# A recurrent unit moved into the projection before it and between the attention's units, and one softmax map handed to ScalarE

## The reference

```python
# block 0: x = x + gate * even_mixer(modulated rms_norm(x))
q, k, v, g_a, x_b, g_b = split(h @ w_in)            # 512 columns each
a_out = diff_attention(q, k, v, t5_table, lam, ...) # 4 heads; softmax(map 0) - lam * softmax(map 1)
b_out = bidir_rglru(x_b, ...)
y = concat([a_out * silu(g_a), b_out * silu(g_b)]) @ w_out

def bidir_rglru(x, ...):
    xc = conv4(x) + conv_b                          # 4 taps along the tokens
    gate_a, gate_x = sigmoid(xc @ w_a + b_a), sigmoid(xc @ w_x + b_x)   # both directions
    log_a = -8 * gate_a * softplus(-lam)
    a, mult = exp(log_a), sqrt(-expm1(2 * log_a))
    u = mult * gate_x * xc
    return forward_scan(a[0], u[0]) + backward_scan(a[1], u[1])   # h = a * h + u

# block 1: odd_mixer: q, k, v, g = split(h @ w_in); 16 heads of windowed attention with a
# softmax over 256 masked, biased scores; (out * silu(g)) @ w_out
```

## Time and profile before

| | us |
|---|---|
| three runs | 2048.07, 2049.44 (median), 2052.09 |
| profiled execution: time, span | 2052.9, 2051.1 |
| busy PE, DVE, ACT, POOL | 1916.6, 1396.5, 689.6, 114.3 |
| mean granted clock of TensorE | 0.970 of full speed |

### The profile page before, as it was taken

How to read it: one execution, slowest core, us unless ns; L and a number is a source line. 1 busy time by engine, 2 the same in 40 slices (tenths; PEclk the granted TensorE clock), 3 DMA queues, 4 the chain that set the end, 5 groups by cost and what they waited for, 6 DMA issues and landing times.

```text
span 2051.1 us, 28124 instructions
## 1 busy us (share of the span) xinstructions
PE 1916.6 (93%) x10810; PEld 1661.7 (81%) x10810; DVE 1396.5 (68%) x2096; ACT 689.6 (34%) x938; POOL 114.3 (6%) x76
## 2 busy tenths in 40 slices
PE   2986899899999999999999999999999999889998
PEld 1965788788888888878888888888888889679998
DVE  7868899976666667667766666676665226776654
ACT  2455355432222124332322222232222124434432
POOL 2001100100000110002000001100000010010000
PEclk9986899899999999999999999999999999999999
DMA  9852855433433443433334434443443223224544
GB/s 378 307 191 59 239 196 185 156 130 146 153 142 133 167 163 127 150 123 126 148 129 151 153 130 162 159 146 133 152 153 107 99 93 142 104 88 140 180 163 156
DMA packets 75749, 315.97 MB, mean 154 GB/s; under 512 B 19060, under 2 KB 22904, under 8 KB 56344
## 3 DMA queue, kind: packets, MB, share of 16 engines
q1 hardware_dynamic: 75136, 314.15, 43.5%
q10 hardware_dynamic: 536, 0.79, 0.1%
HBM read 313.86 MB, written 1.06 MB: 154 GB/s over the span
## 4 chain that ended last, share of the span: by engine, by line
PE 75%; DVE 16%; ACT 3%; issue 3%; POOL 1%; DMA 1%; SPq 0%; DVEq 0%; ACTq 0%; POOLq 0%
PE acc L1542 73%; DVE Wl L933 3%; DVE tmp L919 2%; PE psN L1542 1%; ACT Wh L554 1%; DVE najunk L974 1%; DVE najunk L971 1%; DVE small L1172 1%; DMA afirst<-in_ada_w 1%; DVE psGT L968 1%; DVE XT L919 1%; DVE Hl L919 1%; DVE tmp L1190 1%; DVE psGT L971 1%; DVE Wl L999 1%
## 5 line engine op out<-in xcount | busy, mean ns | idle before, releaser
L1542 PE MATMUL acc<-Hh,Wh 128*128 128x256 f32 (+1 forms) x2464 | 834.7, 339 | 39.9 <-DVE Hl L919 17.9
L1542 PE MATMUL acc<-Hl,Wh 128*128 128x256 f32 (+1 forms) x2464 | 825.2, 335 | 0.0
L1542 PE MATMUL acc<-Hh,Wl 128*128 128x256 f32 (+1 forms) x2464 | 824.9, 335 | 0.0
L933 DVE TENSOR_TENSOR Wl<-raw,Wh 128x2048 fp32r<-128x2048 f32 (+1 forms) x207 | 433.4, 2094 | 239.3 <-ACT Wh L554 239.1
L1542 PEld LDWEIGHTS acc<-Hh,Wh 128*128 128x128 f32 x2464 | 477.8, 194 | 97.2 <-issue 27.2
L1542 PEld LDWEIGHTS acc<-Hl,Wh 128*128 128x128 f32 x2464 | 477.8, 194 | 44.3 <-issue 0.7
L1542 PEld LDWEIGHTS acc<-Hh,Wl 128*128 128x128 f32 x2464 | 477.4, 194 | 43.8
L554 ACT ACTIVATE Wh<-raw 128x2048 fp32r<-128x2048 f32 (+1 forms) x207 | 361.1, 1745 | 330.8 <-PE acc L1542 309.5
L1542 PE MATMUL acc<-hidh,Wh 128*128 128x512 f32 (+1 forms) x770 | 270.4, 351 | 1.4 <-DVE Wl L933 1.3
L1542 PE MATMUL acc<-hidl,Wh 128*128 128x512 f32 (+1 forms) x770 | 269.2, 350 | 0.0
L1542 PE MATMUL acc<-hidh,Wl 128*128 128x512 f32 (+1 forms) x770 | 269.2, 350 | 0.0
(11 more groups left out here) (240 smaller groups left out, 1257.8 us busy)
## 6 DMA issues: line engine op xcount, KB each, us to landing
raw<-in_ffn_up SPq DMA_DIRECT2D x88, 1024.0 KB, 4.9
graw<-in_mod_w SPq DMA_DIRECT2D x144, 512.0 KB, 5.6
raw<-in_ffn_down SPq DMA_DIRECT2D x64, 704.0 KB, 4.1
graw<-in_ada_w SPq DMA_DIRECT2D x32, 512.0 KB, 5.9
raw<-in_odd_in SPq DMA_DIRECT2D x16, 1024.0 KB, 5.0
raw<-in_even_in SPq DMA_DIRECT2D x12, 1024.0 KB, 7.4
raw<-in_conv_in SPq DMA_DIRECT2D x12, 1024.0 KB, 4.9
afirst<-in_ada_w SPq DMA_DIRECT2D x8, 1024.0 KB, 13.1
```

What stands on the lines that cost most here:

```text
L933: nc.vector.tensor_tensor(Wl[:, half, 0:f], raw[:, slot, 0:f], Wh[:, half, 0:f].bitcast(f32), ALU.subtract)\
L1542: return nc.tensor.matmul(out, lhsT, rhs, start=start, stop=stop)
```

## The change

The tiles of `even_in` are taken in another order (`EVEN_TILE`): the two that hold the unit's input x_b first, then v, q, k and the gates. Its loops for SP and TensorE are written out. Convolution, gate products, tanh, decays and the products up to `tT` are done quarter by quarter beside its tiles (`CONV_AT`, `GATES_AT`, `DECAYS_AT` say at which), as are the bias rows, the transposes of v and the sums for lambda. TensorE's gate products stand in the middle of a tile and use the banks `psN` and `psT[1]` in turn. The square root comes before the attention. Between the attention's units VectorE does the recurrence of a quarter (after units 0, 2, 4, 6), the gating (3, 5, 7) and low parts; ScalarE the tanh of the gates and the high parts. The two maps are scaled and biased in one operation, from two banks; the sign is put into that operation and the exponential, so that no operation negates the maximum. The squares and sums of the output's norm are done head by head. The output projection begins with the unit's chunks (`EVEN_CHUNKS`), before the norm is there, and the modulation that stood beside its tile 0 stands before the norm's products. The context's load moves on SP from before the first projection's side loads to behind the projection's. In the second block ScalarE divides map 1 of each unit, VectorE map 0.

The core of the diff:

```diff
-        ctanh = view("ctanh", 76 * KB, [P, 3, D])
+        ctanh = view("ctanh", 76 * KB, [P, D])
+        cbt = tmp[:, :, :].rearrange("p (b a) n -> p b (a n)", b=2)
...
+        pair = [ctx.enter_context(nc.psum_tensor(f"acc{a}", [P, 1024], f32)) for a in range(2)]
+        acc = [[pair[a][:, b * 512:(b + 1) * 512] for b in range(2)] for a in range(2)]
...
+        EVEN_TILE = [8, 9, 4, 5, 0, 1, 2, 3, 6, 7, 10, 11]
+        CONV_AT = {3: 0, 4: 1, 6: 2, 7: 3}
+        GATES_AT = {4: 0, 5: 1, 7: 2, 8: 3}
+        DECAYS_AT = {6: 0, 7: 1, 9: 2, 10: 3}
+        GATE_ORDER = [4 * q + c for c in range(4) for q in range(4)]
+        EVEN_CHUNKS = [4, 5, 6, 7, 0, 1, 2, 3]
...
-            sp.dma_start(XT[:, :, LAT:TOK], A["ctx_t"]).then_inc(ld_ctx, 16)
...
-                tiles(sp, s, PER, LEAD, step, head={"even_in": 1, "odd_in": 4, "conv_in": 3}.get(s.name, 0))
+                tiles(sp, s, PER, LEAD, step, head={"even_in": 3, "odd_in": 4, "conv_in": 3}.get(s.name, 0))
+                if s.name == "even_in":
+                    sp.dma_start(XT[:, :, LAT:TOK], A["ctx_t"]).then_inc(ld_ctx, 16)
...
+                act.wait_ge(diff.taken, g + 1)
+                nc.scalar.activation(otsq[:, g, :], OT[:, g, :], ACT.Square).then_inc(ot_sq, 1)
...
+            def gate_tanh(n):
+                i = GATE_ORDER[n]
+                act.wait_ge(lru_gate, n // 2 * 2 + 2)
+                nc.scalar.activation(gates[:, i // 8, i % 8, :], (psN, psT[1])[n // 2 % 2][:, (n % 2) * LAT:(n % 2 + 1) * LAT],
+                                     ACT.Tanh, scale=0.5, bias=lsc[:, 16 + i:17 + i]).then_inc(ev_thx, 1)
+            def decays(c):
+                act.wait_ge(sp_done, 1)
+                act.wait_ge(ev_thx, 4 * c + 4)
+                for i in (c, 4 + c):
+                    nc.scalar.activation(tT[:, i, :], gates[:, 0, i, :], ACT.Tanh, scale=sp4[:, i:i + 1], bias=sp4[:, i:i + 1])
+                    nc.scalar.activation(aT[:, i, :], gates[:, 0, i, :], ACT.Exp, ...).then_inc(lru_at, 1)
+                act.wait_ge(lru_at, 2 * c + 2)
+                nc.scalar.activation(dirs(gates[:, 0, :, :], c), dirs(aT[:, :, :], c), ACT.Square).then_inc(lru_sq, 1)
             def beside_even_in(t):
...
+                if t - 1 in GATES_AT:
+                    for n in range(4 * GATES_AT[t - 1], 4 * GATES_AT[t - 1] + 4):
+                        gate_tanh(n)
...
+                if t in DECAYS_AT:
+                    decays(DECAYS_AT[t])
...
+            def second_map(u):
+                act.wait_ge(na_rec, u + 1)
+                nc.scalar.activation(PR[:, u % 2, LAT:2 * LAT], PR[:, u % 2, LAT:2 * LAT], ACT.Copy, scale=rec[:, 2 * u + 1:2 * u + 2])\
+                    .then_inc(na_norm1, 1)
...
+                for u in UNITS_AT.get(t, ()):
+                    second_map(u)
                 act.wait_ge(tile_done, s.n0 + t + 1)
...
+                    if a is diff:
+                        ins = stt(x, a.both(u), -a.scale, a.bias(g, qb), ALU.mult, ALU.subtract)
...
-                    link(nc.vector.tensor_reduce(out=out, in_=L[:, u % 2, :, :], op=ALU.max, axis=AX.X))
-                    nc.vector.tensor_scalar(out, out, -1.0, None, ALU.mult).then_inc(a.maxed, 1)
+                    nc.vector.tensor_reduce(out=out, in_=x, op=ALU.min, axis=AX.X).then_inc(a.maxed, 1)
...
+                if a is na:
+                    ins.then_inc(na_rec, 1)
+                    dve.wait_ge(na_rec, u + 1)
+                    nc.vector.tensor_scalar(p[:, 0:LAT], p[:, 0:LAT], r[:, 0:1], None, ALU.mult).then_inc(a.normed, 1)
+                    return
...
+            def conv(c):
...
+            def gated_input(c):
+                dve.wait_ge(lru_xc, c + 1)
+                dve.wait_ge(ev_thx, 4 * c + 4)
+                gx = dirs(gates[:, 1, :, :], c)
+                link(stt(gx, gx, 1.0, xc[:, c:c + 1, :].to_broadcast([P, 2, LAT]), ALU.add, ALU.mult))
+            def one_less_square(c):
+                dve.wait_ge(lru_sq, c + 1)
+                t_ = dirs(tT[:, :, :], c)
+                link(stt(t_, dirs(gates[:, 0, :, :], c), 1.0, t_, ALU.add, ALU.mult))
+            def bounded():
+                nc.vector.tensor_scalar(tT[:, :, :], tT[:, :, :], 1e-30, None, ALU.max).then_inc(lru_m2, 1)
+            def recurrence(c):
...
+                stt(u_, u_, 0.5, dirs(tT[:, :, :], c), ALU.mult, ALU.mult).then_inc(lru_u, 1)
+                dve.wait_ge(lru_u, c + 1)
+                nc.vector.tensor_tensor_scan(h[:, c, :], aT[:, c, :], gates[:, 1, c, :], 0.0, ALU.mult, ALU.add)
+                link(nc.vector.tensor_tensor_scan(h[:, 4 + c, :][:, ::-1], aT[:, 4 + c, :][:, ::-1], gates[:, 1, 4 + c, :][:, ::-1], 0.0,
...
+                nc.vector.tensor_tensor(gates[:, 1, c, :], h[:, c, :], h[:, 4 + c, :], ALU.add).then_inc(lru_hs, 1)
+            def gating(c):
...
+                link(stt(g_, g_, 1.0, ev[:, 8:24, :].rearrange("p (r x) n -> p r x n", x=8)[:, :, 4 + c, :], ALU.add, ALU.mult))
+                stt(gates[:, 1, c, :], gates[:, 1, c, :], 0.5, tT[:, 4 + c, :], ALU.mult, ALU.mult).then_inc(lru_h, 1)
+            def lru_low(c):
...
+            def beside_diff(u):
+                if u % 2 == 0:
+                    recurrence(u // 2)
+                elif u >= 3:
+                    gating(u // 2 - 1)
+                if u in (5, 7):
+                    lru_low(u // 2 - 2)
+            def beside_even_in(t):
+                if t in CONV_AT:
+                    conv(CONV_AT[t])
+                if t == 8:
+                    gated_input(0), gated_input(1), one_less_square(0)
+                if t == 10:
+                    gated_input(2), gated_input(3), one_less_square(1)
+                if t == 11:
+                    one_less_square(2), one_less_square(3), bounded()
...
+                if t == 1:
+                    softplus_argument()
+                if t == 8:
+                    dve.wait_ge(c_tanh, 2)
+                    link(stt(cb[:, :, :], cbt, 1.0, cb[:, :, :], ALU.add, ALU.mult))
+                if t == 5:
+                    softplus()
...
+            attention(diff, beside=beside_diff)
+            gating(3)
+            lru_low(2)
+            lru_low(3)
+            dve.wait_ge(ot_ss, 4)
+            nc.vector.tensor_scalar(means[:, 0:8], psN[:, LAT:LAT + 8], 1.0 / P, EPS, ALU.mult, ALU.add).then_inc(ot_mean, 1)
+            modulation_of(S["even_out"], 0, 0, 0, ejunk)
             dve.wait_ge(ot_spread, 1)
+            for c in range(4):
+                link(stt(OT[:, c, :], OT[:, c, :], lam[:, 5:6], psGT[:, c * LAT:(c + 1) * LAT], ALU.mult, ALU.mult))
+                stt(OT[:, c, :], OT[:, c, :], 0.5, tT[:, c, :], ALU.mult, ALU.mult).then_inc(ev_full, 1)
...
+                if t == 3:
+                    pe.wait_ge(ld_even, 48)
+                    mm(psN[0:4, 0:511], t5in[0:32, 512:516], t5in[0:32, 0:511], True, True).then_inc(t5_ps, 1)
...
+                    if k == 3 and t in GATES_AT:
+                        c = GATES_AT[t]
+                        pe.wait_ge(lru_xc, c + 1)
+                        if c == 0:
+                            pe.wait_ge(t5_cp, 1)
+                        for n in range(4 * c, 4 * c + 4):
+                            if n >= 4 and n % 2 == 0:
+                                pe.wait_ge(ev_thx, n - 2)
+                            mm((psN, psT[1])[n // 2 % 2][...], lruw[:, GATE_ORDER[n], :], xc[:, c, :], True, True)\
+                                .then_inc(lru_gate, 1)
...
+            outsums(3)
+            part(0, range(4))
+            pe.wait_ge(ot_rstd, 1)
             for b in range(8):
+                ins = spread(psGT[:, b * P:(b + 1) * P], rstd, b)
             ins.then_inc(ot_spread, 1)
+            part(1, range(4))
+            part(0, range(4, KC)).then_inc(tile_done, 1)
+            part(1, range(4, KC)).then_inc(tile_done, 1)
```

More of the change, by code:

```diff
@@ L342, in __init__ @@
                     a.score = lambda u, m: acc[u % 2][m][:, 0:keys]
+                    a.both = lambda u: pair[u % 2][:, :].rearrange("p (m n) -> p m n", m=2)[:, :, 0:keys]
                     a.turn_in = lambda u: psT[u % 2]
@@ L792, in _ @@
[L792 to L797 removed]
+            project(S["even_in"], lambda m: ev[:, 2 * EVEN_TILE[m // 2] + m % 2, :], beside_even_in)
@@ L1213, in attention @@
                 maxes(a, 0)
-                if beside:
+                if beside and a is gqa:
                     beside()
@@ L1219, in attention @@
                     normalise(a, u)
+                    if beside and a is diff:
+                        beside(u)
                     if a is gqa and u >= 2 and u % 2 == 0:
@@ L1359, in _ @@
[L1359 to L1365 removed]
+                dve.wait_ge(ev_hi, 5 + c)
@@ L1749, in turn, with outsums @@
                 ins.then_inc(a.turned, 1)
+            def outsums(g):
+                pe.wait_ge(ot_sq, g + 1)
+                for b in range(2):
```

(6 more changed lines are left out.)

282 lines of the change are left out of this document (131 added, 151 removed).

## The result

| | before | after |
|---|---|---|
| median of four runs, us | 2048.89 (2048.07 to 2052.09) | 2029.78 (2029.55 to 2032.98) |
| profiled execution: time, span | 2052.9, 2051.1 | 2032.98, 2031.2 |
| busy PE, DVE, ACT, POOL | 1916.6, 1396.5, 689.6, 114.3 | 1904.1, 1387.5, 700.5, 113.9 |

The ratio is 0.9907, 95% interval 0.9890 to 0.9925: 15.4 to 22.5 us less. A second set of runs of the same two kernels gave 2032.26 against 2047.43, ratio 0.9927 (0.9908 to 0.9946), 11.1 to 18.8 less. The forecast, 16.7 less, lies in both.

The account below looks back on a forecast made before the run. VectorE was taken to bound the first attention and, after tile 6, the changed first projection; VectorE and TensorE share the second attention. Gains 13.2 + 3.55 = 16.7 gave 2032.7 us from the median 2049.4; range 2025 to 2042.

Parts of the forecast that it names:

- part 3: Second block's attention: VectorE loses the sign flip and one division, 0.45 per unit; 3.55 us of 7.2 gained.
- Part 1: Recurrent unit inside the first projection: VectorE never waits from tile 6 on; attention starts at 134.0, 5.5 us gained.
- The shift of tile 6: First projection: bias-row product, four gate products and a short wait bring `Wl` of tile 6 from 77.1 to 79.6.
- Part 2: First attention and what follows: last division at 167.2, first residual at 184.8 instead of 198.0, gain 13.2 us.
- The operation across two banks: Attention unit: one 128x512 operation replaces two on 128x256, taken at 0.74 us, bounds -0.4 to +0.4 per unit.
- Moved, not hidden: Between attention units: the recurrence's scans stand in VectorE's order, so all 12.1 us of moved work counts.
- The modulation of tile 0: Output projection: its 2.8 us hides beside GpSimd's power; without that cover it costs 2.8.
- rival A: Second attention follows VectorE throughout, as TensorE's 73.1 busy us may hold waits; all 7.2 count, 2029 us; chance 0.15.
- B: Moved VectorE work costs more than its rows, or attention units wait for ScalarE; gain 10, 2040 us; chance 0.17.
- C: Clock falls inside the first projection after small TensorE waits; 2067 us with tiles 4 to 11; chance 0.05.
- D: Gain taken back behind the output projection by a load or queue; under 4 us left; chance 0.05.

Follow-up runs that it names:

- `behind`: Changed kernel with the whole recurrence, gatings and low parts placed behind the attention instead of between its units; 2029.71 us.
- `pe_cut`: Changed kernel with 32 of TensorE's 96 products left out in tiles 8 and 10 of the first projection; 2027.72 us.

## Why the prediction was right, step by step

| stretch, us | before | forecast of the difference | after | measured difference |
|---|---|---|---|---|
| `Wl` of tile 2 to the attention | 85.3 to 85.6 | -5.5 | 80.84 to 80.87 | -4.6 |
| attention to the end of its last division | 22.6 | +10.7 | 32.4 | +9.8 |
| last division to first residual | 35.9 to 36.1 | -18.4 | 18.1 to 19.0 | -17.4 |
| second projection | 132.0 to 132.8 | -3.55 | 128.1 to 128.4 | -3.6 to -4.6 |

Ranges are over three profiles before (the second projection's include the kernel without part 3) and five or more after, in all kernels whose part in question is the one or the other. The sum measured is 12.2 and about 4, 16.2 against the forecast 16.7.

*Part 1 held in its mechanism; one term was small.* From `Wl` of tile 6 to the end of VectorE's list 51.5 us passed (79.55 to 131.07), forecast 51.4, with no wait for `Wh` over 0.12. The shift of tile 6 was mis-sized: 26.3 from `Wl` of tile 2 instead of 23.0, so 3.3 and not 2.5. From one `Wl` to the next it took 5.76 before; with the bias-row product 6.89 (1.1 more, forecast 0.9), with the first gate products and the wait ahead of them 7.93 (2.2 more, forecast 1.6). The wait of 1.5 that I had counted for TensorE at tile 10 was 0.41. In the first pair of profiles the changed kernel's tile 2 came 0.9 earlier by chance, and that made the absolute mark, 134.0, look exact. That VectorE alone bounds the stretch was true of the changed kernel and no further: a cut of 4.0 there brings 1.8.

*Part 2 held.* The operation across two banks took 0.68, below the 0.74 taken and inside its bounds; the unit 2.55 instead of 2.64, which is 0.7 of the 0.9 that the attention was shorter. That these 0.9 and the 0.9 that part 1 fell short cancel is luck. The recurrence costs 2.36 (137.92 to 140.28), forecast 2.4. "Moved, not hidden" is what `behind` shows. Behind the division the forecast was 0.5 to 1.4 short: TensorE's half of tile 0 (171.62 to 176.51) and what follows came a few tenths later each. The modulation of tile 0 was covered, with 2.91 us to spare.

*Part 3 held, in its mechanism too.* I let six units count in full and the ten in the middle only with TensorE's 0.85 of idle time. VectorE's `Wl` does gain 0.46 per unit through the middle, 4.0 us by the one at 339.50 before and 321.27 after (100.77 and 96.78 from the first mask operation), but that is a lead over TensorE: the wait of 1.50 at 328.65 takes 1.4 of it back. TensorE itself moves as forecast. Its score products of an early unit of the middle, and those that VectorE then waits for, are, before

```profile
285.32 0.70 PE L1542 MATMUL psGT<-od_proj 64*128 64x256 f32 x4
...
343.40 1.13 PE L1542 MATMUL psGT<-od_proj 64*128 64x256 f32 x8
```

and after

```profile
270.27 0.70 PE L1629 MATMUL psGT<-od_proj 64*128 64x256 f32 x4
...
327.47 1.13 PE L1629 MATMUL psGT<-od_proj 64*128 64x256 f32 x8
```

Between the two 58.08 passed before and 57.20 after: the middle gave TensorE 0.9, close to its idle time. Up to the operation that waits the gain is 2.2 (forecast 1.35 and 0.85), and the last three units give 1.4 (forecast 1.35). So TensorE's 73.05 busy us of 73.9 held next to no waits, and rival A's premise falls with its size.

*The rivals.* A is out by the size of part 3 and by TensorE's own marks. B is out: no unit and no step of the projection was dearer than its rows. C is out: the clock is 1.00 in the whole first stretch, though TensorE waited up to 0.49 us inside its tiles, and waits of 1.46 and 1.37 in `pe_cut` left it at 1.00 too; what the Trainium skill says in the section named for this rival ("TensorE: Matmul & The Clock Gate", "A second HAM failure mode: psum-queue depth-cycling") has no case here. D is out: the gain stays behind the output projection to the end.

*What the forecast left out* is the clock ahead of the norms: 2.0 of the 19.9 us between the first pair of profiles and, by the repeated profiles, chance of either sign. Where the last 1.0 lies was not followed up.

## What to carry to other kernels

Work that is moved inside an engine's own list is priced as a sum over that list, and here that sum was good to 1 us in 50; what it does not tell is how far behind the next engine stands, and cutting one engine's work shows that in one run. Moving the recurrence between the attention's units gained nothing by itself: what gained, by the marks, was the projection's spare time, the shorter operations, and the order of the norm's chain (no run takes these three apart). Where the waits that are left end (2.06 for high parts, 2.91 for a spread), the next order could be read straight from the trace. An engine's lead over the next one is not time saved until that one moves too, so a gain is read where the two meet. Before a difference of 1 to 3 us is explained, profile one of the two kernels twice and count from marks that repeat.
